# A two-layer decoder trunk: norm gains multiplied into prepared weights by GpSimd, and a reordered schedule

## The chip, the cores and the metric

The kernel runs on one core of a Trainium2 chip. The metric is device time in microseconds (us) of one execution; lower is better. The core's engines each run their own queue of instructions in program order: PE (TensorE, the matrix products), ACT (ScalarE), DVE (VectorE), POOL (GpSimd) and SP (SyncE, which here only issues DMA transfers). They meet only in semaphores: an instruction that waits holds up everything behind it on its engine.

## The reference

The input x is 1024 positions by 1024 features, mem is 256 by 1024. There are two layers, all in float32, and both have the same frame:

```
h = rms_norm(x, norm_gains[l, 0]); z = h @ w_in[l]
y_main = pool_mixer(z_main, ...)         # layer 0: sliding means over 2, 4, 8, 16 positions
y_main = dilated_mixer(z_main, shared)   # layer 1: 12 heads, rotary q, windows (128,1),(512,4),(2048,16)
y_mem  = memory_attn(z_mem, mem, mem_norm[l], w_mem_kv[l])   # 4 heads, kv = rms_norm(mem, g) @ w_mkv
y = concatenate([y_main, y_mem]) @ w_out[l];  x = x + rms_norm(y, norm_gains[l, 1])
h = rms_norm(x, norm_gains[l, 2]); gu = h @ w_gate_up[l]     # 1024 x 5632
y = (silu(gu[..., :D_FF]) * gu[..., D_FF:]) @ w_down[l];  x = x + rms_norm(y, norm_gains[l, 3])
# after layer 0: shared K, V = rope(rms_norm(x, kv_norm) @ w_kv), 1024 x 1536, one for all groups
```

`rms_norm(x, g)` is x over the root of its mean square, times the gains g, one for each feature. A gain can be multiplied into the rows of the weight matrix that follows instead of into x; the kernel does that for the matrices named below.

## The kernel before

**Precision.** Each factor of a matrix product is split into a high part H (the value rounded to the type fp32r) and a low part L = value - H, and a product is the sum of three matmuls, H*H, L*H and H*L. So each weight matrix that comes from memory needs two vector operations ahead of its first matmul: a copy with rounding (ACT, `WH<-WR` or `VH<-VR`) and a subtraction (DVE or POOL, `WL<-WR,WH` or `VL<-VR,VH`).

**Jobs.** The work of PE is a hand-written list of jobs (`plan_jobs`), one for each 128-wide stripe of an output: `mem` (memory keys and values), `in`, `kv`, `pool`, `out`, `ffn`, `st`, `down`. A job with a tag h covers one half (512) of the positions. A job's `slot` says where its weights lie in the shared weight space, and so when they can be loaded: once the previous user of the space is through. `HOOKS` lists the places k in a job at which one step of the attention (scores, softmax, transposes, values) is put between the job's matmuls.

**Norm statistics.** DVE sums the squares of x into `SS`; two small PE jobs called "col" (`PX<-CN,SS`, L688) and "row" (`PX<-CN,RC`, L697) turn them into the row `RSTD`. A wait of PE for `SS` is a wait for the last square to be summed. `mv` (L741) is PE's transposition of the memory values.

**FFN by Strassen's scheme.** Of the FFN's gate and up matrices the first stripes are ordinary `ffn` jobs; the other 18 stripes of each layer are 18 "pairs" (`st` jobs, `pair(l, f)`). A pair computes a 2x2 block product with 7 block products instead of 8. Each block product is 4 k-tiles of 3 matmuls, so a pair is 84 matmuls of 128x512 (L875, L876, L877). The weights of pair q+1 are prepared while PE works on pair q, in this order:

- `st_add(q+1)`, in layer 0 on DVE: four sums of blocks in `SR` (L1877 to L1880), the fourth ends `st_added`
- ACT: `st_raw_hi(q+1)` (L1252, 128x1536) rounds the plain blocks, `st_sum_hi(q+1)` (L1257, 128x2048) the sums; the second waits for `st_added`
- DVE: `st_raw_lo(q+1)` (L1887), `st_sum_lo(q+1)` (L1894), each after its high part; PE's first product of pair q+1 waits for the second

Between them DVE combines the block products of pair q as they end: u2 (L1900), c11 (L1906), u3 (L1911), c22 and v2 (L1917, L1918), c21 (L1922), c12 (L1927), each with one factor in PSUM, and ACT does the gate's nonlinearity in two halves (`silu_first` L1263, `silu_second` L1269).

**Prepared weights.** The 24 weight matrices (128x1024 each) of layer 1's `mem`, `in` and `kv` jobs are prepared during 16 of layer 0's 18 pairs, by turns one and two in a pair (`prepared(f)`), and stored back to memory. For each: SP loads it into one of three `VR` buffers, `keep_weight` on ACT multiplies in the gains `GN` (8 operations of 128x128, one for each k, L1141) and rounds it (L1144), POOL subtracts (L2390), SP stores `VH` and `VL`. POOL has no other work in layer 0's pairs. ACT's order in a pair is `p1_copy`, `silu_first`, `keep_weight` once or twice, `st_raw_hi(q+1)`, `st_sum_hi(q+1)`:

```
                    p1_copy(q)
                    if l == 0:
                        silu_first(q)
                        for i in prepared(f):
                            keep_weight(i)
                    if f < NF - 1:
                        st_raw_hi(q + 1)
                        st_sum_hi(q + 1)
```

**The other places that the change touches.** The start of layer 0: two `in` jobs (query stripes 6, 7), four `mem` jobs, then the pooled `in` jobs, with the memory attention in the hooks. The start of layer 1: `mem` jobs, for which the row `RSTDM` (the memory's norm) comes back from memory, then `in` jobs 6 and 7 in halves. Layer 1's output product in two parts (features 0 to 511 and 512 to 1023), with the rest of the attention in the hooks of part 0; the attention ends with a combination of its three groups (`combine_last`). Then layer 1's sublayer: `add_y` (L1848) adds the parts, `residual` (L1630) makes the new x, `scaled_low` (L1641) its low part `BL`, while PE is in `ffn` jobs, whose weights are split by ACT and DVE (`weight_lo`, L1578).

## Time and profile before

| what | value |
|---|---|
| time, median of 3 runs | 2398.61 us (2392.47 to 2398.93) |
| the profiled execution: its own time | 2402.4 us |
| its span | 2400.4 us |
| its mean granted clock of TensorE | 0.955 |
| PE busy | 2202.2 us, 92% |
| DVE busy | 1264.6 us, 53% |
| ACT busy | 944.5 us, 39% |
| POOL busy | 328.0 us, 14% |

PE is busy nearly all the time, so what can be gained without taking matmuls away is in PE's idle time and in the stretches in which its granted clock is below full. The profile gives for each idle stretch of an engine the instruction that ended it. The granted clock is one of two levels, 1.2 and 2.4 GHz; a value between them is a mean over a stretch.

### The profile page before, as it was taken

To read this page: it belongs to the slowest core of one execution; us is meant where nothing else is said; L and a number is where in the kernel's file an instruction comes from. 1 tells how busy PE (TensorE), PEld (TensorE's weight loads), DVE (VectorE), ACT (ScalarE), POOL (GpSimd) and SP (SyncE) were. 2 spreads that over 40 slices of the span, in tenths; PEclk is the share of its full clock that TensorE was granted. 3 is DMA by queue.
4 is the path that set the end of the run, shared out by engine and by line. 5 is a ranking of instruction groups with operands and counts; after the bars stand their busy time and mean duration, and the time that the engine had idled before them with its cause. 6 is when DMAs were issued, how large, how long until landed. Compare 5 with 4: busy or idle time off the path is not lost.

```text
span 2400.4 us, 25623 instructions
## 1 busy us (share of the span) xinstructions
PE 2202.2 (92%) x9718; PEld 1766.8 (74%) x9718; DVE 1264.6 (53%) x1901; ACT 944.5 (39%) x1575; POOL 328.0 (14%) x198
## 2 busy tenths in 40 slices
PE   6897999888888999998999997979799999999996
PEld 5675888776767778887777765657578888878885
DVE  6354375655565643525344445466656666672442
ACT  5335352434344433322444446653542222242421
POOL 3432100112111000000000014022222222200000
PEclk8998999999899999998999999989899999999998
DMA  4202232344444635554111101004212222263543
GB/s 160 73 14 90 88 121 75 142 184 149 179 148 173 222 117 199 163 174 182 53 64 43 59 30 36 19 17 154 75 53 79 79 79 82 94 216 97 197 132 104
DMA packets 83210, 265.10 MB, mean 110 GB/s; under 512 B 9360, under 2 KB 10640, under 8 KB 77840
## 3 DMA queue, kind: packets, MB, share of 16 engines
q1 hardware_dynamic: 66960, 234.10, 27.8%
q10 hardware_dynamic: 16128, 29.37, 3.6%
q8 instruction: 77, 1.26, 0.2%
q14 instruction: 45, 0.37, 0.0%
HBM read 195.14 MB, written 68.29 MB: 110 GB/s over the span
## 4 chain that ended last, share of the span: by engine, by line
PE 70%; DVE 12%; ACT 9%; issue 5%; DMA 3%; SPq 1%; POOL 0%; ACTq 0%; DVEq 0%
PE PS L662 8%; PE PS L875 7%; PE PS L877 7%; PE PS L876 7%; PE PS L663 7%; PE PS L665 7%; PE PS L895 6%; PE PS L897 6%; PE PS L896 6%; PE PSC L803 3%; ACT VR L1141 2%; PE PO L777 2%; DVE SL L1894 2%; PE PTR L787 1%; ACT VH L1144 1%
## 5 line engine op out<-in xcount | busy, mean ns | idle before, releaser
L895 PE MATMUL PS<-IH,DH 128*128 128x512 f32 x704 | 276.6, 393 | 6.5 <-DVE IL L1975 6.0
L897 PE MATMUL PS<-IH,DL 128*128 128x512 f32 x704 | 275.3, 391 | 0.0
L896 PE MATMUL PS<-IL,DH 128*128 128x512 f32 x704 | 275.3, 391 | 0.0
L875 PE MATMUL PS<-BH,SH 128*128 128x512 f32 x432 | 179.1, 415 | 54.7 <-DVE SL L1894 51.6
L875 PE MATMUL PS<-BHT,SH 128*128 128x512 f32 x576 | 225.8, 392 | 0.0
L876 PE MATMUL PS<-BLT,SH 128*128 128x512 f32 x576 | 224.2, 389 | 0.0
L877 PE MATMUL PS<-BHT,SL 128*128 128x512 f32 x576 | 224.2, 389 | 0.0
L876 PE MATMUL PS<-BL,SH 128*128 128x512 f32 x432 | 176.7, 409 | 0.0
L877 PE MATMUL PS<-BH,SL 128*128 128x512 f32 x432 | 176.7, 409 | 0.0
L895 PEld LDWEIGHTS PS<-IH,DH 128*128 128x128 f32 x704 | 132.9, 189 | 36.7 <-DVE IL L1975 8.5
L897 PEld LDWEIGHTS PS<-IH,DL 128*128 128x128 f32 x704 | 133.0, 189 | 27.9
L896 PEld LDWEIGHTS PS<-IL,DH 128*128 128x128 f32 x704 | 133.0, 189 | 27.5
L875 PEld LDWEIGHTS PS<-BH,SH 128*128 128x128 f32 x432 | 85.8, 199 | 79.6 <-DVE SL L1894 61.8
L1578 DVE TENSOR_TENSOR DL<-DR,DH 128x1408 fp32r<-128x1408 f32 x64 | 103.8, 1624 | 73.0 <-ACT DH L1004 73.0
L662 PE MATMUL PS<-XH,WH 128*128 128x512 f32 x320 | 138.8, 434 | 0.0
L663 PE MATMUL PS<-XL,WH 128*128 128x512 f32 x320 | 128.7, 402 | 0.0
L875 PEld LDWEIGHTS PS<-BHT,SH 128*128 128x128 f32 x576 | 109.4, 190 | 23.0
L876 PEld LDWEIGHTS PS<-BLT,SH 128*128 128x128 f32 x576 | 109.4, 190 | 23.0
L1613 DVE TENSOR_TENSOR SS<-SS,SCR 128x512 f32<-128x512 f32 x28 | 19.4, 691 | 202.6 <-ACT SCR L1031 202.6
L877 PEld LDWEIGHTS PS<-BHT,SL 128*128 128x128 f32 x576 | 108.1, 188 | 23.0
L662 PE MATMUL PS<-BH,WH 128*128 128x512 f32 x256 | 104.7, 409 | 20.9 <-DVE WL L1578 13.4
L2390 POOL TENSOR_TENSOR VL<-VR,VH 128x1024 fp32r<-128x1024 f32 x24 | 57.9, 2411 | 470.4 <-ACT VH L1144 470.4
(281 smaller groups left out, 4645.2 us busy)
## 6 DMA issues: line engine op xcount, KB each, us to landing
DR<-in_wdn SPq DMA_DIRECT2D x64, 704.0 KB, 4.1
SR<-in_wst SPq DMA_DIRECT2D x36, 1024.0 KB, 4.8
IR<-inner SPq DMA_DIRECT2D x88, 256.0 KB, 4.9
WR<-in_w SPq DMA_DIRECT2D x36, 512.0 KB, 4.6
inner<-TP SPq DMA_DIRECT2D x36, 512.0 KB, 2.6
VR<-in_w SPq DMA_DIRECT2D x24, 512.0 KB, 4.1
w_keep<-VH SPq DMA_DIRECT2D x24, 512.0 KB, 3.7
w_keep<-VL SPq DMA_DIRECT2D x24, 512.0 KB, 4.6
```

The source lines that it names most:

```text
L662: MM(out[h], wh[:, i, :], rh(h, k), start=(i == 0), stop=False)
L663: MM(out[h], wh[:, i, :], rl(h, k), start=False, stop=False)
L665: ins = MM(out[h], wl[:, i, :], rh(h, k), start=False, stop=last)
L803: MM(score_bank(a)[:, 0:nk], QF[rows, t, P * n:P * (n + 1)], keys, start=True, stop=True).then_inc(scored, 1)
L875: MM(BANK[bank], SH[b][:, w, c], BH[t][:, k, :], start=(k == 0), stop=False)
L876: MM(BANK[bank], SH[b][:, w, c], BL[t][:, k, :], start=False, stop=False)
L877: ins = MM(BANK[bank], SL[b][:, w, c], BH[t][:, k, :], start=False, stop=(k == 3))
L895: MM(bank, wh[:, i, :], IH[r][:, :], start=(k == 0), stop=False)
L896: MM(bank, wh[:, i, :], IL[r][:, :], start=False, stop=False)
L897: ins = MM(bank, wl[:, i, :], IH[r][:, :], start=False, stop=(k == NF - 1))
L1578: V.tensor_tensor(lo(j), raw(j), as_f32(hi(j)), ALU.subtract).then_inc(w_lo_dve, 1)
L2390: G_.tensor_tensor(VL[i % NV][:, :, :], VR[i % NV][:, :, :], as_f32(VH[i % NV][:, :, :]), ALU.subtract).then_inc(v_lo, 1)
```

## The change

Five parts. None changes what is computed, and the number of matmuls is the same.

1. **Prepared weights.** POOL multiplies the gains into a prepared weight, in one operation with `GN` broadcast along the row, ahead of its subtraction; ACT only rounds. On ACT `st_raw_hi(q+1)` moves ahead of `silu_first(q)`, and the second weight of a pair behind `st_sum_hi(q+1)`.
2. **Start of layer 0.** The first pooled `in` job moves ahead of the four `mem` jobs, with the norm's col and row hooks in it, and the squares ahead of the memory's split; the attention's hooks are spread anew; SP issues the loads of the next two `in` jobs behind the stores of the memory's parts.
3. **Start of layer 1.** `RSTDM` is loaded during the down product instead of behind two large loads; `mv` moves from the first half's `in` job 7 to the second half's.
4. **Output product of layer 1, part 0.** Attention steps: 4 in each job of the first half and 1 in each of the second (before 3 or 2, and 4, 4, 2, 2, 2, 2, 2, 1); the combination's pieces start earlier and are spread.
5. **Layer 1's sublayer.** `ffn` jobs get other slots, so that the first four weights are loaded and split during the output product's part 1; the product of y with the norm's row (16 operations, `y_norm`) moves from POOL to DVE (as in layer 0); the col and row hooks of x's second half move from the second `ffn` job of the second half to the first; pairs and down jobs of layer 1 use the weight space's regions in another turn.

```diff
@@ plan_jobs
             run = [Job("in", 0, m) for m in (6, 7)]
+            run += [Job("in", 0, POOL_IN[0])]
             run += [Job("mem", 0, m, gain=8) for m in range(4)]
-            run += [Job("in", 0, m) for m in POOL_IN]
+            run += [Job("in", 0, m) for m in POOL_IN[1:]]
...
-        jobs += [Job("ffn", l, (f, j), halves=(h,), tag=h, slot=wide(2 * f + j),
+        jobs += [Job("ffn", l, (f, j), halves=(h,), tag=h, slot=2 * f + j if l else wide(2 * f + j),
...
@@ attention steps
-        for m in range(NMT):
-            HOOKS[J[("in", 0, m, None)]] = (1, 3, 5, 7)
+        for n, m in enumerate(POOL_IN):
+            HOOKS[J[("in", 0, m, None)]] = () if n == 0 else (4, 5, 6, 7) if n == 1 else (1, 2, 4, 5, 7)
...
-            HOOKS[J[("out", 1, m, (0, 0))]] = (1, 2, 3) if m < 5 else (1, 3)
-            HOOKS[J[("out", 1, m, (0, 1))]] = (0, 1, 2, 3) if m < 2 else (1, 3) if m < 7 else (1,)
+            HOOKS[J[("out", 1, m, (0, 0))]] = (0, 1, 2, 3)
+            HOOKS[J[("out", 1, m, (0, 1))]] = (1,)
@@ PE
-                              (1, 0, 1): {3: [("col", s_x, 1)], 7: [("row", s_x, 1)]}}
+                              (1, 0, 0): {0: [("col", s_x, 1)], 4: [("row", s_x, 1)]}}
...
-                places = {0: [("col", 4, 1)], 3: [("row", 4, 1)]} if h else {4: [("mv", 1, 0)]}
+                places = {0: [("col", 4, 1)], 3: [("row", 4, 1)], 6: [("mv", 1, 0)]} if h else {}
@@ ACT keep_weight
-                act.wait_ge(v_loaded[b], 16 * (i // NV + 1))
-                for k in range(KT):
-                    ins = A(VR[b][:, k, :], VR[b][:, k, :], ACT.Copy, scale=GN[:, 8 * o.gain + k:8 * o.gain + k + 1])
-                    ins.then_inc(v_gained, 1)
-                act.wait_ge(v_gained, KT * (i + 1))
+                act.wait_ge(v_gained, i + 1)
                 A(VH[b][:, :, :], VR[b][:, :, :], ACT.Copy).then_inc(v_hi, 1)
@@ ACT pair
                     p1_copy(q)
+                    ready = prepared(f) if l == 0 else ()
+                    if len(ready):
+                        keep_weight(ready[0])
+                    if f < NF - 1:
+                        st_raw_hi(q + 1)
                     if l == 0:
                         silu_first(q)
-                        for i in prepared(f):
-                            keep_weight(i)
                     if f < NF - 1:
-                        st_raw_hi(q + 1)
                         st_sum_hi(q + 1)
+                    if len(ready) > 1:
+                        keep_weight(ready[1])
@@ DVE residual, layer 1
-                if r != 3:
-                    V.tensor_tensor(y, y, RSTD[:, c], ALU.mult).then_inc(y_normed[h], 1)
+                V.tensor_tensor(y, y, RSTD[:, c], ALU.mult).then_inc(y_normed[h], 1)
@@ DVE output product, part 0
+                    if (h, m) == (0, 7):
+                        combine_last(0)
+                        combine_last(1)
+                    if h and m in (1, 2, 4, 6):
+                        combine_last((2, 3, 4, 5)[(1, 2, 4, 6).index(m)])
...
@@ POOL
             for i in range(len(PRE)):
+                o = JOBS[PRE[i]]
+                pool.wait_ge(v_loaded[i % NV], 16 * (i // NV + 1))
+                G_.tensor_tensor(VR[i % NV][:, :, :], VR[i % NV][:, :, :], GN[:, 8 * o.gain:8 * o.gain + KT]
+                                 .unsqueeze(2).to_broadcast([P, KT, P]), ALU.mult).then_inc(v_gained, 1)
                 pool.wait_ge(v_hi, i + 1)
...
-            y_norm(0)
-            y_norm(1)
@@ SP
+                        sp.dma_start(RSTDM[:, :], rstd_keep).then_inc(mem_back, 16)
...
-            sp.dma_start(RSTDM[:, :], rstd_keep).then_inc(mem_back, 16)
```

The first place is ACT's queue in a pair of layer 0 with two prepared weights. Before (`SCR` is `p1_copy`; the rows of `TP` are `silu_first` and, last, the pair before's or this pair's `silu_second`; `VR_192` and `VR_193` are the two weights):

```order
L1279 ACTIVATE SCR_71<-PS 128x512
L1263 ACTIVATE TP_91<-TP_91 128x512
L1141 ACTIVATE VR_192<-VR_192,GN 128x128 x8
L1144 ACTIVATE VH_198<-VR_192 128x1024
L1141 ACTIVATE VR_193<-VR_193,GN 128x128 x8
L1144 ACTIVATE VH_199<-VR_193 128x1024
L1252 ACTIVATE SH_204<-SR_200 128x1536
L1257 ACTIVATE SH_204<-SR_200 128x2048
L1269 ACTIVATE TP_91<-TP_91 128x512
L1279 ACTIVATE SCR_71<-PS 128x512
```

The same place of the kernel after (all of its line numbers are higher; L1262 is the former L1252, L1267 the former L1257):

```order
L1289 ACTIVATE SCR_71<-PS 128x512
L1153 ACTIVATE VH_198<-VR_192 128x1024
L1262 ACTIVATE SH_204<-SR_200 128x1536
L1273 ACTIVATE TP_91<-TP_91 128x512
L1267 ACTIVATE SH_204<-SR_200 128x2048
L1153 ACTIVATE VH_199<-VR_193 128x1024
L1279 ACTIVATE TP_91<-TP_91 128x512
```

The rounding of the plain blocks (128x1536) stands behind one copy instead of behind sixteen gain operations, two copies and `silu_first`, and that of the sums (128x2048) ahead of the second weight.

The second place is POOL's queue in the same pairs. Before, the last two splits of ordinary weights (`WL`) and three prepared weights:

```order
L2347 TENSOR_TENSOR WL_141<-WR_115,WH_167 128x1024
L2347 TENSOR_TENSOR WL_142<-WR_116,WH_168 128x1024
L2390 TENSOR_TENSOR VL_194<-VR_191,VH_197 128x1024
L2390 TENSOR_TENSOR VL_195<-VR_192,VH_198 128x1024
L2390 TENSOR_TENSOR VL_196<-VR_193,VH_199 128x1024
```

After, the same stretch:

```order
L2377 TENSOR_TENSOR WL_141<-WR_115,WH_167 128x1024
L2377 TENSOR_TENSOR WL_142<-WR_116,WH_168 128x1024
L2424 TENSOR_TENSOR VR_191<-VR_191,GN 128x1024
L2427 TENSOR_TENSOR VL_194<-VR_191,VH_197 128x1024
L2424 TENSOR_TENSOR VR_192<-VR_192,GN 128x1024
L2427 TENSOR_TENSOR VL_195<-VR_192,VH_198 128x1024
L2424 TENSOR_TENSOR VR_193<-VR_193,GN 128x1024
L2427 TENSOR_TENSOR VL_196<-VR_193,VH_199 128x1024
```

Each subtraction now has the product with the gains ahead of it, in the same buffer.

The third place is PE's queue at the start of the second half of layer 1's `ffn` jobs. Before, in the second job (`BH_223` and `BH_224` are k = 0 to 3 and 4 to 7 of the second half's x, `WH_170` the second job's weight):

```order
L662 MATMUL PS<-BH_223,WH_170 128x512
L663 MATMUL PS<-BL_231,WH_170 128x512
L665 MATMUL PS<-BH_223,WL_144 128x512
L688 MATMUL PX<-CN,SS 128x1 x4
L662 MATMUL PS<-BH_224,WH_170 128x512
```

After, in the first job (`WH_165` is its weight, `WH_172` that of the first half's last job):

```order
L669 MATMUL PS<-BH_222,WH_172 128x512
L670 MATMUL PS<-BL_230,WH_172 128x512
L672 MATMUL PS<-BH_222,WL_146 128x512
L669 MATMUL PS<-BH_223,WH_165 128x512
L670 MATMUL PS<-BL_231,WH_165 128x512
L672 MATMUL PS<-BH_223,WL_139 128x512
L695 MATMUL PX<-CN,SS 128x1 x4
L669 MATMUL PS<-BH_223,WH_165 128x512
```

The col hook (`PX<-CN,SS`) moved ahead by 11 k-steps of three matmuls: PE now meets it behind the second half's first k-step.

## Rows read from the trace of the kernel before

**Rows 1.** The page, a group of instructions: busy us, mean ns, idle before, releaser.
```profile
L875 PE MATMUL PS<-BH,SH 128*128 128x512 f32 x432 | 179.1, 415 | 54.7 <-DVE SL L1894 51.6
```

**Rows 2.** Chain that ended last, layer-0 pairs: start us, us, what.
```profile
430.81 2.21 DVE SL L1894
...
789.38 2.21 DVE SL L1894
```

**Rows 3.** Windows: us, then busy (x instructions) PE PEld DVE ACT POOL, clock, DMA share, GB/s.
```profile
430.81:789.38 358.57, 309.25 (x1264) 249.00 (x1262) 199.90 (x226) 153.92 (x282) 55.45 (x23) 0.93 0.44 163
2000.00:2100.00 100.00, 100.00 (x443) 82.81 (x442) 64.38 (x64) 26.33 (x22) 25.81 (x20) 1.00 0.25 90
```

**Rows 4.** Timeline, PE at two pair starts: start us, us, instruction [idle before <-releaser].
```profile
480.74 0.50 PE L875 MATMUL PS<-BH,SH 128*128 128x512 f32 x1 [1.50 <-DVE SL L1894]
...
505.01 0.80 PE L875 MATMUL PS<-BH,SH 128*128 128x512 f32 x1 [4.94 <-DVE SL L1894]
```

**Rows 5.** Timeline, ACT within the pair that starts at 480.74.
```profile
490.48 2.44 ACT L1141 ACTIVATE VR<-VR,GN 128x128 f32<-128x128 f32 x8
492.96 1.06 ACT L1144 ACTIVATE VH<-VR 128x1024 fp32r<-128x1024 f32 x1
...
497.35 1.47 ACT L1252 ACTIVATE SH<-SR 128x1536 fp32r<-128x1536 f32 x1
498.73 1.90 ACT L1257 ACTIVATE SH<-SR 128x2048 fp32r<-128x2048 f32 x1
```

**Rows 6.** Timeline, DVE within the same pair.
```profile
492.00 0.69 DVE L1880 TENSOR_TENSOR SR<-SR 128x512 f32<-128x512 f32 x1
...
498.86 2.70 DVE L1887 TENSOR_TENSOR SL<-SR,SH 128x1536 fp32r<-128x1536 f32 x1 [5.56 <-ACT SH L1252]
...
502.68 2.28 DVE L1894 TENSOR_TENSOR SL<-SR,SH 128x2048 fp32r<-128x2048 f32 x1
```

**Rows 7.** Groups of instructions by line, POOL: busy us, mean ns, idle before.
```profile
L2390 POOL TENSOR_TENSOR VL<-VR,VH 128x1024 fp32r<-128x1024 f32 x24 | 57.9, 2411 | 470.4 <-ACT VH L1144 470.4
...
L2422 POOL TENSOR_TENSOR YOA<-YOA,RSTD 128x512 f32<-128x512 f32 x16 | 25.4, 1619 | 73.8 <-ACT RSTD L1022 73.8
...
L2341 POOL TENSOR_TENSOR WR<-WR,GN 128x1024 f32<-128x1024 f32 x4 | 9.5, 2387 | 19.2 <-DVE XLA L1597 19.2
```

**Rows 8.** Timeline, POOL within the same pair.
```profile
497.53 2.42 POOL L2390 TENSOR_TENSOR VL<-VR,VH 128x1024 fp32r<-128x1024 f32 x1 [1.02 <-ACT VH L1144]
```

**Rows 9.** Source lines, DVE: count, duration ns min/median/max, first and last start.
```profile
L1887 DVE TENSOR_TENSOR SL<-SR,SH x36: 1750/1756/2700, 399.0 to 2107.4; 128x1536 fp32r<-128x1536 f32 x36
...
L1605 DVE TENSOR_TENSOR SS<-SS,TP x7: 1212/2729/3185, 28.3 to 41.8; 128x1024 f32<-128x1024 f32 x7
```

**Rows 10.** Timeline, PE at the start of layer 0.
```profile
44.58 1.87 PE L688 MATMUL PX<-CN,SS 128*128 128x1 f32 x8 [7.05 <-DVE SS L1605]
...
72.44 0.76 PE L803 MATMUL PSC<-KM,QF 64*128 64x256 f32 x1 [5.90 <-ACT VM L1087]
```

**Rows 11.** Timeline, PE at the start of layer 1.
```profile
1084.90 0.58 PE L728 MATMUL PSC<-MH,WH 128*128 128x256 f32 x1 [3.16 <-DMA RSTDM<-rstd_keep]
...
1115.87 1.11 PE L741 MATMUL PX<-CN,MV 128*128 128x128 f32 x4 [4.74 <-DVE MV L1692]
```

**Rows 12.** Timeline, PE ahead of layer 1's first output products.
```profile
1616.60 0.77 PE L662 MATMUL PS<-CH,WH 128*128 128x512 f32 x1 [8.92 <-DVE CL L1814]
```

**Rows 13.** Timeline, PE in layer 1's FFN, first half.
```profile
1717.44 0.79 PE L662 MATMUL PS<-BH,WH 128*128 128x512 f32 x1 [9.91 <-DVE WL L1578]
...
1728.69 0.50 PE L662 MATMUL PS<-BH,WH 128*128 128x512 f32 x1 [3.23 <-DVE WL L1578]
```

**Rows 14.** Timeline, DVE in the same stretch.
```profile
1712.16 1.75 DVE L1630 SCALAR_TENSOR_TENSOR YOA<-YOA,GN,TP 128x512 f32<-128x512 f32 x1
...
1719.23 0.74 DVE L1630 SCALAR_TENSOR_TENSOR YOA<-YOA,GN,TP 128x512 f32<-128x512 f32 x1
...
1729.15 0.68 DVE L1613 TENSOR_TENSOR SS<-SS,TP 128x512 f32<-128x512 f32 x1
```

More of the change, by code:

```diff
@@ L820, in _ @@
             job(J[("in", 0, 7, None)], xh, xl)
-            memory_job(0, 0, hook=at_k({6: [("col", 0, 0), ("col", 0, 1)]}))
-            memory_job(0, 1, hook=at_k({4: [("row", 0, 0), ("row", 0, 1)], 7: [("mcol", 0, 0)]}))
-            memory_job(0, 2, hook=at_k({6: [("mrow", 0, 0)]}))
+            job(J[("in", 0, POOL_IN[0], None)], xh, xl,
+                hook=at_k({3: [("col", 0, 0)], 4: [("col", 0, 1)], 7: [("row", 0, 0), ("row", 0, 1)]}))
+            memory_job(0, 0, hook=at_k({1: [("mcol", 0, 0)]}))
+            memory_job(0, 1, hook=at_k({3: [("mrow", 0, 0)]}))
+            memory_job(0, 2)
             memory_job(0, 3)
@@ L827, in _, with hook @@
                 j = J[("in", 0, m, None)]
-                def hook(i, first=n == 0, places=HOOKS[j]):
-                    if first and i == 0:
+                if n == 0:
+                    continue
+                def hook(i, first=n == 1, places=HOOKS[j]):
+                    if first and i == 2:
                         memory_values(0, 0)
@@ L1163, in _ @@
                     weight_hi(1)
+            weight_hi(2)
+            for k in range(KT):
+                square0(k)
             act.wait_ge(tables_in, MEM_IN)
@@ L1462, in _ @@
             sub_layer(0)
-            for k in range(6):
-                residual(2, 1, k)
-            memory_values(1)
-            for k in range(6, KT):
+            for k in range(KT):
                 residual(2, 1, k)
@@ L1493, in combine @@
                 else:
-                    for g, t in enumerate(tiles):
-                        act.wait_ge(cmb_out, 3 * pair + g + 1)
-                        A(CH[:, t, :], OF[:, t, :], ACT.Copy).then_inc(c_hi, 1)
+                    act.wait_ge(cmb_out, 3 * pair + g + 1)
+                    A(CH[:, tiles[g], :], OF[:, tiles[g], :], ACT.Copy).then_inc(c_hi, 1)
             def split_memory(m):
@@ L1514, in _ @@
                         step()
-                    if (n, q) in ((15, 4), (16, 1), (17, 1)):
-                        combine(0, n - 15)
+                    if n == 15 and 2 <= q <= 4:
+                        combine(0, "exp", q - 2)
+                    if (n, q) == (16, 1):
+                        combine(0, "inverse")
+                    if n == 17 and q <= 2:
+                        combine(0, "split", q)
                     if n and i != 1 and q < 4:
@@ L1765, in _, with pooled_input @@
             query0(7)
+            def pooled_input(n):
+                j = J[("in", 0, POOL_IN[n], None)]
+                dve.wait_ge(mm_done, j + 1)
+                if n == 0:
+                    dve.wait_ge(pads_zero, 3)
+                    for h in range(2):
+                        ins = V.tensor_tensor(T[0][:, HALF[h]], BANK[banks(j)[h]], RSTD[:, HALF[h]], ALU.mult)
+                    ins.then_inc(in_scaled, 1)
+                else:
+                    V.tensor_tensor(T[0], PS[j % 2][:, :], RSTD[:, :], ALU.mult).then_inc(in_scaled, 1)
+            pooled_input(0)
             for m in range(4):
@@ L2274, in combine_last @@
                 else:
-                    for n, t in enumerate(tiles):
-                        split_low(t, 18 + n + 1)
-                    split_low(7, 22)
+                    split_low(tiles[part - 5], 18 + part - 4)
             for n in range(19):
@@ L2362, in _ @@
             pool.wait_ge(x0_lo, KT)
-            gain(POOL_JOBS[0])
-            weights_to(first + 3)
+            weight_lo(POOL_JOBS[0])
+            done[0] += 1
+            pool.wait_ge(ss0_done, KT)
+            gain(POOL_JOBS[1])
+            weights_to(J[("in", 0, POOL_IN[3], None)])
             pool.wait_ge(pads_zero, 3)
@@ L2416, in _ @@
             weights_to(NJ)
-            def y_norm(h):
-                pool.wait_ge(px_free, px_at[("row", 5, h)])
-                for k in range(KT):
-                    G_.tensor_tensor(YO[h][:, k, :], YO[h][:, k, :], RSTD[:, HALF[h]],
-                                     ALU.mult).then_inc(y_normed[h], 1)
             def st_add(q):
-                b = SR[q % 2]
+                b = SR[pair_slot(q)]
                 pool.wait_ge(*st_seen(q))
```

132 lines of the change are left out of this document (68 added, 64 removed).

## The prediction

> **What bounds the kernel now.** I read the page first: PE is busy 92% of the span, so only its idle and half-clock stretches can be won. The costliest idle entry of the page is PE's wait at the first product of a pair, 54.7 us, of which 51.6 us ended with DVE's `st_sum_lo`, L1894 [rows 1]. The chain of waits says the same for layer 0: `st_sum_lo` stands in it 16 times, from 430.81 to 789.38, so 15 pairs take 358.57 us, 23.90 us each [rows 2]. The windows give what a pair should take: in layer 1, 443 matmuls in 100.00 us without any idle time, so 84 matmuls are 18.96 us; in layer 0 the mean granted clock is 0.93 over the pairs, against 1.00 there [rows 3]. A layer-0 pair thus loses 4.94 us, and there are 16 with weights to prepare.
>
> The timeline divides the loss. PE waits 1.50 us ahead of the pair that starts at 480.74 and 4.94 us ahead of the next, at 505.01, where its first matmul takes 0.80 us instead of 0.50 [rows 4]. The two waits make 6.4 of the 9.9 us that two pairs lose; the other 3.5 us are matmuls at the half clock after the long wait.
>
> Why `st_sum_lo` is late is read inside the pair that starts at 480.74, one with two weights. ACT gives them 2 x (2.44 + 1.06) = 7.0 us from 490.48 on, and only then, at 497.35 and 498.73, rounds the next pair's blocks (1.47 and 1.90 us) [rows 5]. DVE had its sums ready at 492.7, then idled 5.56 us for ACT, did `st_raw_lo` in 2.70 us and `st_sum_lo` at 502.68, 21.9 us after the pair's start [rows 6]. So ACT's order and its eight small gain products are the cause.
>
> **Part 1, the pairs.** Counted from the pair's first product (t = 0). ACT no longer does the gains: of 3.5 us for a weight 1.06 stay. The rounding of the plain blocks comes behind one copy and is done long before DVE asks. The sums are ready at 492.69 - 480.74 = 11.95 [rows 6]; ACT rounds them in 1.90 [rows 5], to about 13.9. DVE meanwhile has u3 and `st_raw_lo`, which takes 1.76 us alone and took up to 2.70 [rows 9], to about 15; then c22 and v2, then `st_sum_lo` from 15.9. The 2.28 us of it [rows 6] end at 18.2, ahead of 18.96: no stall, if nothing else is in its way.
>
> What is in its way is POOL. Its load in a two-weight pair is now 4 operations of 2.4 us (the subtraction's mean is 2411 ns; the nearest row for the product with broadcast gains is L2341's, the same shape, 2387 ns [rows 7]), 9.6 us of 19. The trace shows what two engines do to each other: the only `st_raw_lo` that take 2.70 instead of 1.76 us are those beside a POOL subtraction, as at 498.86 beside the one that runs from 497.53 to 499.95: 1.08 us of overlap, 0.94 us longer [rows 6, 8, 9]. The square sums L1605 take 1.21 us at best and 2.73 in the median where POOL works beside them [rows 9]. So a DVE operation with two SBUF inputs waits for a POOL operation that is under way. In a two-weight pair ACT's second copy now stands behind the sums' rounding, 13.9 + 1.06 = 14.9, and POOL's second subtraction runs from there to 17.4. `st_sum_lo`, ready at 15.9, would end at 17.4 + 2.3 = 19.7 or somewhat later: a stall of 0.7 to 1.0 us. In a one-weight pair POOL's 4.8 us mostly lie earlier: 0 to 0.6 us. The long wait that brought the half clock is gone, so those 3.5 us for two pairs go too. I take 19.4 us for the mean pair: 16 x (23.9 - 19.4) = **-72 us**. Bounds: no contention at all, 16 x 4.94 = -79; every other pair pays a whole further POOL operation (2.4 us) and some half clock, 21.0 us on the mean, -46.
>
> The Trainium skill's page "SBUF — State Buffer", section "Who interferes with whom", gives this a rule: the port that DVE uses for a second SBUF input is shared with GpSimd, and is held exclusively by an instruction that has it. By it `st_sum_lo` waits out the whole subtraction, as I took it; the trace agrees with its 0.94 us of delay for 1.08 us of overlap. The same rule speaks against this change, since it doubles GpSimd's share of the port in these pairs; what it could cost at most is the second rival.
>
> **Part 2, start of layer 0.** PE waits 7.05 us for the square sums and 5.90 us for the memory values [rows 10]. After, the first pooled `in` job (about 11 us at full clock) fills the first wait, and the memory products come later; but two `in` weights are now loaded only behind the memory's stores, and PE will wait for the next job's weight, I estimate 8 us, from the load's place in SP's queue. I lay out both orders to the point where PE resumes: 72.4 before with 7/8 of the pooled job to do, about 72 after with all of it done. That gives -10 less a half-clock stretch: **-8 us**; bounds 0 (waits only renamed) and -13 (both waits gone).
>
> **Part 3, start of layer 1.** The 3.16 us wait for `RSTDM` falls to the 1 to 1.5 us that the memory's own reload takes, and the 4.74 us wait of `mv` goes, as `MV` is then long ready [rows 11]; each also had matmuls at half clock behind it. Against that, the col hook of the second half's first `in` job, which `mv` no longer delays, meets the squares of x about 4 us early. **-6 us**, bounds -2 and -9.
>
> **Part 4, output product.** PE waits 8.92 us for the last low part of the attention's output (`CL`) [rows 12], at the end of a chain that starts only with the last attention steps. With four steps a job in the first half the chain starts about two jobs earlier, some 10 us, so this wait and some 6 us of smaller ones in the hooks before it go, while denser steps give back a little: **-15 us**, bounds -9 (only the one wait) and -20.
>
> **Part 5, layer 1's sublayer.** The waits for `WL` of 9.91 and 3.23 us go [rows 13], since the first four weights are split an output part earlier. POOL's `y_norm` took 1.62 us each [rows 7], and beside it DVE's `residual` took 1.75 instead of 0.74 us [rows 14]; on DVE the 16 products are some 11 us, which the faster `residual` and `scaled_low` (16 x 2 x 1.0, at most) pay for. So the second half's x comes at about the same time as before, its last square at 1729.2 [rows 14], which after is met by a col hook that PE reaches 11 k-steps (about 7 us) sooner [order of PE, third place], with PE's waits gone besides: a new wait of 7 to 8 us and some half clock after it. Together 13.1 + 6 (smaller waits, half clock) + 13 (the row's values, and with them the chain into the pairs, no longer wait on late hooks) less 11: **-21 us**, bounds -8 and -28.
>
> **Sum.** -72 - 8 - 6 - 15 - 21 = -122 us. The profiled execution's own time is 2402.4, 3.8 above the median of the runs, 2398.61. So 2280 in its terms, 2277 in the median's; I say **2278 us**. With the bounds of part 1 and half of those of the others this case spans 2262 to 2296.
>
> **The rivals.**
> - *Contention is dearer* (0.18). If POOL's product or subtraction meets the four sums as well (they have two SBUF inputs, and end at 11.95), everything behind them slips by up to 2.4 us, and `st_sum_lo` by another 2.4: pairs of 21.5 us, a gain of 38 instead of 72 us, 2312 us. For it: the doubled POOL time. Against: the sums come at a point where the first subtraction is done.
> - *Only the pairs gain* (0.14): in parts 2 to 5 each wait that goes is replaced by the next in line, as the new waits on `in` weights and squares already suggest. 2402 - 72 - 12 = 2318, less 4: 2314 us.
> - *Better than forecast* (0.07): no stall in the pairs, and parts 2 to 5 at their far bounds: -79 - 13 - 9 - 20 - 28 = -149, 2250 us.
> - *The change doesn't do what it says in the pairs* (0.04): ACT, with its copy ahead of the plain blocks, waits there for POOL's product, because a weight lands late; pairs stay near 23.9, and only the rest gains: 2350 us. Against: ACT found its weight there at 490.48 with no wait, and a weight is loaded a pair ahead.
> - *Slower* (0.02): POOL and DVE become the bound of a pair. The price is the sum of what excludes one another: 9.6 us of POOL, 2.9 of sums, 1.8 + 2.3 of low parts and 0.7 of the product, some 17 us; with DVE's seven PSUM operations of 0.7 added as if nothing overlapped, 22.6. It turns the sign only where the pair takes over 23.9 + 50/16 = 27 us, that is if POOL's product took 7 us or more instead of 2.4, say by a slow form of the broadcast: 2402 + 16 x 5 = above 2420 with the other parts at nothing. L2341 has the same form at 2.387 us [rows 7], which is why I give it so little.
>
> **How the numbers follow.** The forecast has 0.55. From 2252 to 2320 the range holds it, most of the two rivals with 0.18 and 0.14 and some of the better case; 0.15 is left out. A measurement of this kernel can tell about 0.3% (7 us) from no change. All cases but the last are faster by more than that; same has 0.01, slower 0.02.
>
> **What the profile after would show.** Right: PE's wait on `st_sum_lo` falls from 51.6 to under 15 us, the pairs' chain has a period near 19.4, the granted clock in them is near 1.0; `st_sum_lo` at about 4 us instead of 2.3 in every other pair; POOL's new product near 2.4 us; no wait on `WL` or `CL`, but waits of 7 to 8 us on an `in` weight at the start and on `SS` in the ffn jobs. Wrong: sums of 2 us instead of 0.7 (first rival), ACT idle ahead of its first copy (fourth), waits of the same sum under other names in parts 2 to 5 (second). What I am least sure of is parts 4 and 5, where many short waits and the clock's answer to them make up the term.

## The result and the profile after

| | before | after |
|---|---|---|
| time, median | 2397.72 us (2392.47 to 2398.93, 4 runs) | 2289.61 us (2289.42 to 2291.11, 4 runs) |
| ratio | | 0.9554, 95% interval 0.9538 to 0.9571 |
| span of the profiled execution | 2400.4 us | 2287.3 us |
| mean granted clock of TensorE | 0.955 | 0.977 |

The change saved 108 us. From the page of the kernel after, the busy times of the engines and the row that answers to [rows 1]:

```profile
PE 2163.1 (95%) x9718; PEld 1739.8 (76%) x9718; DVE 1269.6 (56%) x1918; ACT 888.4 (39%) x1383; POOL 363.2 (16%) x206
...
L888 PE MATMUL PS<-BH,SH 128*128 128x512 f32 x432 | 170.2, 394 | 5.5 <-DVE SL L1923 5.5
```

PE's wait at a pair's first product fell from 54.7 to 5.5 us, and its busy time from 2202 to 2163 us with the same 9718 matmuls, because fewer ran at the half clock of 1.2 GHz: the mean granted clock rose from 0.955 to 0.977.

The spans differ by 113 us, 5 more than the medians, because the profiled execution of the kernel before was 4.7 us above its median (2402.4 against 2397.72). Where the 113 us came from is read by cutting both traces at the same matmuls. In layer 0 a stage begins with the first product of its kind: "start" is all up to layer 0's output product, "pairs 0" begins with the first product of the pairs and ends with the first of the down product. "Down 0 and start 1" reaches to the first dilated score of layer 1, "attention" from there to the last `in` product. From there on a stage begins with the last product of the kind before it, so "pairs 1" begins with the last ffn product. The same cuts in every run serve the experiments below (us):

| stage | before | after | difference |
|---|---|---|---|
| start | 220.9 | 217.3 | -3.6 |
| layer 0, output and ffn | 191.5 | 191.6 | +0.1 |
| **pairs 0** | 420.8 | 353.4 | **-67.4** |
| down 0 and start 1 | 374.6 | 368.8 | -5.8 |
| attention | 279.6 | 273.7 | -5.9 |
| output 1 | 172.4 | 164.2 | -8.2 |
| ffn 1 | 124.6 | 108.7 | -15.9 |
| pairs 1 | 348.7 | 342.8 | -5.9 |
| down 1 | 267.3 | 266.8 | -0.5 |

The pairs first. Their stage in the windows of before and of after (length, busy PE, granted clock, then DMA):

```profile
412.40:833.20 420.80, 368.75 (x1514) 0.94 0.47 171
```

```profile
408.90:762.30 353.40, 347.48 (x1513) 1.00 0.56 204
```

PE's idle time fell by 46 us (52.1 to 5.9), and its busy time by 21 us at a clock that is now full. The chain of waits holds `st_sum_lo` (now L1923) only in every other pair, the ones with two weights:

```profile
448.78 4.08 DVE SL L1923
...
487.41 4.08 DVE SL L1923
...
719.31 4.08 DVE SL L1923
```

From 448.78 to 719.31 are 14 pairs, 19.32 us each, against 23.90 in [rows 2]. Within a pair with two weights, DVE's timeline (the fourth sum, `st_raw_lo`, `st_sum_lo`; last, `st_sum_lo` of the next pair, which has one weight) and then POOL's:

```profile
444.63 0.69 DVE L1909 TENSOR_TENSOR SR<-SR 128x512 f32<-128x512 f32 x1
...
445.83 1.75 DVE L1916 TENSOR_TENSOR SL<-SR,SH 128x1536 fp32r<-128x1536 f32 x1
...
448.70 4.15 DVE L1923 TENSOR_TENSOR SL<-SR,SH 128x2048 fp32r<-128x2048 f32 x1
...
468.29 3.05 DVE L1923 TENSOR_TENSOR SL<-SR,SH 128x2048 fp32r<-128x2048 f32 x1
```

```profile
438.03 2.40 POOL L2427 TENSOR_TENSOR VL<-VR,VH 128x1024 fp32r<-128x1024 f32 x1 [12.41 <-ACT VH L1153]
440.38 1.89 POOL L2424 TENSOR_TENSOR VR<-VR,GN 128x1024 f32<-128x1024 f32 x1
448.30 2.41 POOL L2427 TENSOR_TENSOR VL<-VR,VH 128x1024 fp32r<-128x1024 f32 x1 [6.02 <-ACT VH L1153]
450.65 3.95 POOL L2424 TENSOR_TENSOR VR<-VR,GN 128x1024 f32<-128x1024 f32 x1
```

These answer to [rows 6] and [rows 8]. `st_raw_lo` follows the sums without idle time; before, DVE idled 5.56 us for ACT there. But `st_sum_lo`, started at 448.70 when POOL's subtraction of 448.30 was under way, took 4.15 instead of 2.28 us: POOL's ended at 450.71, and 450.71 + 2.28 = 452.99, where it ended at 452.85. POOL's next product, which takes 1.89 us when alone (440.38), in its turn took 3.95. The `st_sum_lo` of the pairs with one weight is delayed as well, to 2.84 to 3.76 us from 468.29 to 700.19: at 468.29 it met POOL's product for the next weight, under way from 467.29 to 469.19. PE doesn't wait for it there, so only the other pairs stand in the chain. PE at the starts of two pairs, against [rows 4]:

```profile
431.88 0.80 PE L888 MATMUL PS<-BH,SH 128*128 128x512 f32 x1 [3.73 <-DVE SL L1923]
...
452.90 0.50 PE L888 MATMUL PS<-BH,SH 128*128 128x512 f32 x1 [0.22 <-DVE SL L1923]
```

The steady wait, at each later pair start that waits, is 0.22 us; only the first wait of the series has 3.73 us, more than the 1.50 us of [rows 4]. The waits of the other parts in PE's timeline, in order of time, against [rows 10 to 13]:

```profile
68.44 0.80 PE L669 MATMUL PS<-XHA,WH 128*128 128x512 f32 x1 [6.31 <-POOL WL L2377]
...
115.66 0.44 PE L794 MATMUL PTR<-CN,PR 128*128 128x128 f32 x2 [1.83 <-DVE PR L1740]
...
1013.01 0.39 PE L735 MATMUL PSC<-MH,WH 128*128 128x256 f32 x1 [2.63 <-DMA ML<-mem_keep]
...
1048.48 0.72 PE L695 MATMUL PX<-CN,SS 128*128 128x1 f32 x5 [3.72 <-DVE SS L1632]
...
1526.45 0.47 PE L669 MATMUL PS<-CH,WH 128*128 128x512 f32 x1 [1.07 <-POOL WL L2377]
...
1529.28 0.50 PE L669 MATMUL PS<-CH,WH 128*128 128x512 f32 x1 [0.51 <-DVE CL L1843]
...
1599.67 0.59 PE L695 MATMUL PX<-CN,SS 128*128 128x1 f32 x2 [3.30 <-DVE SS L1632]
...
1630.87 1.44 PE L695 MATMUL PX<-CN,SS 128*128 128x1 f32 x6 [4.89 <-DVE SS L1632]
```

At the start the waits of 7.05 and 5.90 us went, one of 6.31 us for the low part of the second pooled job's weight came, and the denser hooks now wait 1.83 us for a probability tile at a time. The wait for `RSTDM` became one of 2.63 us for the memory's low parts, and `mv`'s 4.74 us became 3.72 us for the squares. The 8.92 us for `CL` became 1.07 + 0.51. The waits of 9.91 and 3.23 us for `WL` went, and the squares of both halves of x are waited for, 3.30 and 4.89 us.

### The profile page after: what moved, and what is told of

Same layout as the page of the kernel before. It is cut to its first block, busy times and chain, and to the rows that moved or that the text cites. A ratio compares the mean times of both kernels' runs of the same rounds, so it can differ in the third digit from the quotient of the medians.

```text
span 2287.3 us, 25459 instructions
## 1 busy us (share of the span) xinstructions
PE 2163.1 (95%) x9718; PEld 1739.8 (76%) x9718; DVE 1269.6 (56%) x1918; ACT 888.4 (39%) x1383; POOL 363.2 (16%) x206
## 4 chain that ended last, share of the span: by engine, by line
PE 78%; DVE 11%; ACT 4%; issue 4%; DMA 3%; SPq 0%; POOL 0%; ACTq 0%; DVEq 0%
PE PS L669 8%; PE PS L888 8%; PE PS L889 8%; PE PS L890 8%; PE PS L670 7%; PE PS L672 7%; PE PS L908 7%; PE PS L910 6%; PE PS L909 6%; PE PSC L812 3%; PE PO L784 2%; DVE SL L1923 2%; PE PTR L794 1%; DMA TP<-x_mid 1%; DVE SS L1632 1%
## 5 line engine op out<-in xcount | busy, mean ns | idle before, releaser
L908 PE MATMUL PS<-IH,DH 128*128 128x512 f32 x704 | 276.5, 393 | 5.7 <-DVE IL L2004 5.2
L888 PE MATMUL PS<-BH,SH 128*128 128x512 f32 x432 | 170.2, 394 | 5.5 <-DVE SL L1923 5.5
L889 PE MATMUL PS<-BL,SH 128*128 128x512 f32 x432 | 168.9, 391 | 0.0
L890 PE MATMUL PS<-BH,SL 128*128 128x512 f32 x432 | 168.6, 390 | 0.0
L1632 DVE TENSOR_TENSOR SS<-SS,SCR 128x512 f32<-128x512 f32 x28 | 19.4, 692 | 203.0 <-ACT SCR L1044 203.0
L888 PEld LDWEIGHTS PS<-BHT,SH 128*128 128x128 f32 x576 | 108.1, 188 | 22.6
L1730 DVE CUSTOM_DVE_ANT_0 PSC<-PSC,MK 128x128 f32<-128x128 f32 (+1 forms) x88 | 32.2, 366 | 157.1 <-PE PSC L812 157.0
L2377 POOL TENSOR_TENSOR WL<-WR,WH 128x1024 fp32r<-128x1024 f32 (+2 forms) x40 | 81.1, 2040 | 197.2 <-ACT WH L1017 197.2
L1267 ACT ACTIVATE SH<-SR 128x2048 fp32r<-128x2048 f32 x36 | 69.1, 1920 | 106.4 <-POOL SR L2462 67.9
```

The lines of the kernel that those rows point to most:

```text
L888: MM(BANK[bank], SH[b][:, w, c], BH[t][:, k, :], start=(k == 0), stop=False)
L889: MM(BANK[bank], SH[b][:, w, c], BL[t][:, k, :], start=False, stop=False)
L890: ins = MM(BANK[bank], SL[b][:, w, c], BH[t][:, k, :], start=False, stop=(k == 3))
L908: MM(bank, wh[:, i, :], IH[r][:, :], start=(k == 0), stop=False)
L1267: A(SH[pair_slot(q)][:, S3:, :], SR[pair_slot(q)][:, S3:, :], ACT.Copy).then_inc(st_hi, 1)
L2377: G_.tensor_tensor(lo(j), raw(j), as_f32(hi(j)), ALU.subtract).then_inc(w_lo_pool, 1)
```

## The experiments

All were timed beside the kernel before on the same chip. "Pairs 0" and so on are the stages of the table above, read from the profiled execution of each.

**1. Does the pairs' part stand alone?** The kernel before with part 1 whole.

> The kernel before with part 1 alone (gains on POOL, new order on ACT; start, layer 1 and everything else as before). Theory: the five parts add up, and the pairs are worth what the two traces show between the first matmul of the pairs and the first of the down product, 67 us: 2397.7 - 67 = 2331 us, within 5. Rival, the parts help one another (loads or clock): under 2322 or above 2340.

2329.19 us (ratio 0.9711, 0.9695 to 0.9727); pairs 0: 352.9 us, all other stages within 1 us of before. So the pairs are worth 68 us alone and 67 in the whole change: the parts add.

**2. Was it the order or the gains?** The kernel before with this alone:

```diff
                     p1_copy(q)
+                    ready = prepared(f) if l == 0 else ()
+                    if len(ready):
+                        keep_weight(ready[0])
+                    if f < NF - 1:
+                        st_raw_hi(q + 1)
                     if l == 0:
                         silu_first(q)
-                        for i in prepared(f):
-                            keep_weight(i)
                     if f < NF - 1:
-                        st_raw_hi(q + 1)
                         st_sum_hi(q + 1)
+                    if len(ready) > 1:
+                        keep_weight(ready[1])
```

> The kernel before with ACT's new order in the pairs alone; ACT still multiplies the gains in 8 operations, POOL only subtracts. Theory A, the order was the cause: the first weight takes ACT 3.5 us before t = 7, the sums are rounded at 13.9 to 14.5, the second weight's 3.5 us lie behind it, and POOL's subtraction of it comes after the sums' low part, so pairs of 18.96 to 19.1 us, a saving of 70 to 74 us: 2326 us. Rival B, the gains' 2.44 us on ACT were the cause: pairs stay above 22 us, 2365 us or more.

2321.16 us (ratio 0.9676, 0.966 to 0.9692); pairs 0: 344.4 us, 8.5 less than with the gains on POOL as well. PE waits for `st_sum_lo` only once in the whole stage, and no instance of it (L1898 here: count, ns min/median/max, first and last start) is delayed:

```profile
434.08 0.50 PE L875 MATMUL PS<-BH,SH 128*128 128x512 f32 x1 [0.66 <-DVE SL L1898]
```

```profile
L1898 DVE TENSOR_TENSOR SL<-SR,SH x36: 2279/2284/2286, 404.2 to 2028.9; 128x2048 fp32r<-128x2048 f32 x36
```

18 pairs at 18.96 us are 341.3, so nearly nothing is left to gain. The steady pairs take 19.04 us each, by the starts of `st_sum_lo` (14 pairs from 449.80 to 716.35). Theory A holds: the new order suffices, and ACT has room for the gains. That the products' time on ACT had no part in the old delay does not follow; experiment 4 bears on that.

**3. The gains on POOL without the order.** The kernel before with `keep_weight` and POOL's loop as after, ACT's pair as before.

> The kernel before with the gains on POOL and ACT's old order. Theory A: the sums' rounding slips only by two copies (2.1 us) and the plain blocks' by the same, but POOL's subtractions now fall beside the sums and the low parts on DVE: pairs of about 21 and 19 us by turns, 20.2 in the mean, 2397.7 - 16 x 3.7 = 2339 us. Rival B, the gains were all of it: 2330 us or less.

2403.72 us, a ratio of 1.0024 (1.0013 to 1.0035): slightly slower than before. Pairs 0: 424.8 us. Both theories missed. ACT's timeline in a pair with two weights (two copies, then the plain blocks and the sums), POOL's and DVE's (third and fourth sum, `st_raw_lo`, `st_sum_lo`):

```profile
494.43 1.04 ACT L1140 ACTIVATE VH<-VR 128x1024 fp32r<-128x1024 f32 x1
500.50 1.06 ACT L1140 ACTIVATE VH<-VR 128x1024 fp32r<-128x1024 f32 x1 [5.03 <-POOL VR L2387]
501.47 1.47 ACT L1248 ACTIVATE SH<-SR 128x1536 fp32r<-128x1536 f32 x1
502.84 1.89 ACT L1253 ACTIVATE SH<-SR 128x2048 fp32r<-128x2048 f32 x1
```

```profile
495.55 2.62 POOL L2390 TENSOR_TENSOR VL<-VR,VH 128x1024 fp32r<-128x1024 f32 x1 [15.94 <-ACT VH L1140]
498.13 2.34 POOL L2387 TENSOR_TENSOR VR<-VR,GN 128x1024 f32<-128x1024 f32 x1
501.64 2.40 POOL L2390 TENSOR_TENSOR VL<-VR,VH 128x1024 fp32r<-128x1024 f32 x1 [1.17 <-ACT VH L1140]
```

```profile
495.22 0.69 DVE L1875 TENSOR_TENSOR SR<-SR 128x512 f32<-128x512 f32 x1
495.94 2.77 DVE L1876 TENSOR_TENSOR SR<-SR 128x512 f32<-128x512 f32 x1
...
502.97 2.69 DVE L1883 TENSOR_TENSOR SL<-SR,SH 128x1536 fp32r<-128x1536 f32 x1 [3.66 <-ACT SH L1248]
...
506.78 2.79 DVE L1890 TENSOR_TENSOR SL<-SR,SH 128x2048 fp32r<-128x2048 f32 x1
```

ACT waits 5.03 us ahead of its second copy, for a product with the gains (498.13) that stands on POOL behind the first subtraction (495.55); and behind ACT's second copy stand the roundings. The fourth sum, beside POOL's subtraction, took 2.77 instead of 0.69 us.

**4. The same with POOL's products one weight ahead,** to take ACT's wait away: the product of weight i+1 is issued before the subtraction of weight i.

> As the run with POOL's gains and ACT's old order, but POOL multiplies the next weight's gains before it subtracts the present one, so that ACT never waits for them. Theory A, ACT's 5.03 us wait for the second product with the gains, behind POOL's first subtraction, undid the change there: pairs of about 21 and 19 us by turns, 2397 - 59 = 2339 us, at most 2355. Rival B, the port is what costs (sums and low parts on DVE delayed by POOL whatever its order): 2380 us or more.

2349.15 us (ratio 0.9805, 0.9785 to 0.9825); pairs 0: 376.7 us. So of the 80 us of the pairs between experiments 3 and 2, POOL's own order held 48. Against the kernel before, the pairs are 44 us shorter with ACT's order left as it was: the gain products on ACT were a good part of the delay, and moving them off ACT takes away more than half of it without reordering ACT. DVE's timeline shows what the port held of the rest:

```profile
489.56 2.78 DVE L1876 TENSOR_TENSOR SR<-SR 128x512 f32<-128x512 f32 x1
...
492.87 3.25 DVE L1883 TENSOR_TENSOR SL<-SR,SH 128x1536 fp32r<-128x1536 f32 x1
...
497.24 3.27 DVE L1890 TENSOR_TENSOR SL<-SR,SH 128x2048 fp32r<-128x2048 f32 x1
```

Against 0.69, 1.75 and 2.28 us alone these are 4.6 us more in one pair. Theory A holds for the most part; the mean pair was (376.7 - 344.4)/16 = 2.0 us above the one of experiment 2. How much of that is the port and how much ACT's old order is not separated.

**5. The gains back on ACT in the kernel after,** in the new order.

> The kernel after with the gains back on ACT (8 operations each), in the new order. Theory A: with the order right ACT has room for them, and the 0.36 us a pair that POOL's port use costs goes: 2289.6 - 6 = 2284 us, st_sum_lo at 2.28 us throughout. Rival B: without POOL's product the pairs fall back to above 22 us: 2335 us or more. Rival C, both fit and contention costs nothing: 2289 to 2291 us.

2280.3 us (ratio 0.9513, 0.9498 to 0.9527), 9 us less than the kernel after, the intervals apart. Pairs 0: 344.2 against 353.4 us, every other stage within 2 us, and `st_sum_lo` never delayed:

```profile
L1927 DVE TENSOR_TENSOR SL<-SR,SH x36: 2279/2284/2286, 400.6 to 1989.8; 128x2048 fp32r<-128x2048 f32 x36
```

Of the 9.2 us, 4 are the 14 steady pairs, 19.04 us each as in experiment 2 instead of 19.32; the rest is the first wait, 0.62 instead of 3.73 us, with the half clock behind it. Theory A holds, with a saving of 9 us where 6 were expected.

**6. POOL's second subtraction moved out of DVE's way.** The kernel after, in which POOL does

```diff
+                f, n = next((f, list(prepared(f)).index(i)) for f in range(NHT, NF) if i in prepared(f))
+                if n:
+                    pool.wait_ge(st_lo, 2 * (f - NHT + 2))
                 pool.wait_ge(v_hi, i + 1)
```

> The kernel after; POOL waits for the sums' low part on DVE before it subtracts the second weight of a pair. Theory A, the port is all that the steady pairs still lose (0.22 us of PE's wait and the lateness behind it in every other pair): st_sum_lo takes 2.28 us everywhere, pairs of 18.96 us, 2289.6 - 15 x 0.36 = 2284 us. Rival B: POOL's work, pushed into the next pair, makes ACT wait for the next product with the gains ahead of the plain blocks, and the pairs grow: 2295 us or more.

2283.19 us (ratio 0.9526, 0.9512 to 0.954). Pairs 0: 349.0 us, 4.4 less than after. Of all waits of PE for `st_sum_lo` the first alone is left:

```profile
433.63 0.73 PE L888 MATMUL PS<-BH,SH 128*128 128x512 f32 x1 [3.77 <-DVE SL L1923]
```

The steady pairs take 19.04 us here too (14 pairs from 450.56 to 717.12), so the steady loss was the overlap with POOL's second subtraction, and it could be moved away without undoing anything: theory A. Its other half missed: `st_sum_lo` takes 2.28 us only in the pairs with two weights, and still 2.79 to 3.40 us in the others, where PE doesn't wait for it.

**7. The products with the norm's row back on POOL,** in the kernel after (layer 1's `y_norm`).

> The kernel after with the 16 products of y with the norm's row in layer 1 back on POOL. Theory A, the move to DVE pays, as residual beside POOL took 1.75 instead of 0.74 us: 5 to 10 us slower, 2295 to 2300 us, the waits for SS longer than 3.30 and 4.89 us. Rival B, DVE's 11 us and POOL's contention are worth the same: 2288 to 2291 us. Rival C: DVE is the bound there and POOL takes work off it: 2285 us or less.

2294.6 us (ratio 0.9575, 0.9559 to 0.9591). Ffn 1: 111.2 against 108.7 us. PE's wait for the second half's squares grew from 4.89 to

```profile
1633.19 1.86 PE L695 MATMUL PX<-CN,SS 128*128 128x1 f32 x8 [7.89 <-DVE SS L1632]
```

so theory A holds in sign, with 2.5 us by the stage. The medians differ by 5 us, but the intervals of the two ratios overlap (0.9538 to 0.9571 for the kernel after).

**8. The hooks of x's second half back in the second job,** in the kernel after.

> The kernel after with the col and row hooks of x's second half where they were, in the second ffn job of the second half. Theory A, the earlier hook only made a wait: PE's 4.89 us for SS go, and some of the 6.8 us at half clock behind it, and nothing later waits for the row: 2289.6 - 5 to 8 = 2283 us. Rival B: the row comes some 7 k-steps later, the chain into the pairs is late and PE waits at the first pair for as much: 2289 us or more.

2295.94 us (ratio 0.958, 0.9563 to 0.9596). The wait for the second squares went, as theory A says, and others came, as B says:

```profile
1646.49 0.65 PE L704 MATMUL PX<-CN,RC 128*128 128x128 f32 x4 [0.57 <-DVE RC L1602]
...
1665.88 0.77 PE L669 MATMUL PS<-BH,WH 128*128 128x512 f32 x1 [2.38 <-DVE TP L1857]
...
1686.61 0.76 PE L888 MATMUL PS<-BH,SH 128*128 128x512 f32 x1 [2.69 <-DVE TP L1870]
```

Ffn 1 and pairs 1 together: 105.6 + 347.0 = 452.6, against 108.7 + 342.8 = 451.5 us after. The hook's place is worth 1 us, little more than the same stages vary by in two executions of the kernel after (experiment 11). The rest of the 6 us of the median doesn't come from it: the trace of this run is already 8.5 us behind at the end of output 1, in stages that the edit doesn't touch.

**9. The `in` weight's load ahead of the memory's stores** in SP's queue, in the kernel after.

> The kernel after with the load of the second pooled in job's weight ahead of the stores of the memory's parts in SP's queue. Theory A: PE's wait of 6.31 us for the weight's low part at 68.44 goes or falls under 2 us, with the half clock behind it: 2280 to 2284 us. Rival B: the load waits for its buffer anyway, and the stores wait behind it: 2288 us or more.

2286.07 us (ratio 0.9539, 0.9522 to 0.9556). The start is 212.8 us, 4.5 less, and the wait of 6.31 us is gone. The time fell by less than theory A's 2280 to 2284 us and stayed under rival B's 2288; its interval overlaps that of the kernel after, so by the medians alone nothing is shown.

**10. Both edits of 5 and 9 together.**

> The kernel after with both edits that helped it: gains on ACT in the new order (saved 9) and the second pooled in job's load ahead of the memory's stores (saved 3.5 to 4.5). Theory, they lie in stages of their own and add: 2289.6 - 13 = 2276 us, first stage near 213 us, pairs of layer 0 near 344 us. Rival, the clock takes back what the start gains: 2280 us.

2278.57 us (2274.33 to 2285.16; ratio 0.9506, 0.9478 to 0.9534), the lowest of all, but no less than experiment 5 alone by what can be measured. Pairs 0: 344.6 us; the start, though, took 217.7. The wait of 6.31 us is gone here too. The same two stretches of the start's attention, by windows (busy PE, granted clock), in experiment 9 and then in this one:

```profile
133.66:154.18 20.52, 18.68 (x89) 1.00 0.04 10
154.18:178.24 24.06, 16.88 (x79) 0.92 0.05 17
```

```profile
133.49:155.59 22.10, 20.26 (x89) 0.92 0.03 10
155.59:182.79 27.20, 20.02 (x78) 0.82 0.05 15
```

The matmuls are the same, and the waits ahead of them are too (1.84 and 7.18 us), but the second run had a lower granted clock and took 4.7 us longer. That the load's move saves 4.5 us is thus shown up to 134 us of the run, and what reaches the end is not settled.

**11. The kernel after once more, as a control.**

> The kernel after, unchanged, as a control beside the others: 2288 to 2292 us. Theory: in stages that nothing touches, such as layer 1's attention stage (273.7 us in its first trace, 273 to 280 in the other runs), the time varies by some us with where the clock falls, so an edit's worth is read by its stage.

2290.12 us (2288.22 to 2293.18; ratio 0.9558, 0.9542 to 0.9574), each stage within 0.7 us of the first trace. The attention stage, which no edit touches, took 273.7 and 274.1 us in it, 279.6 to 279.7 in the kernel before and in experiments 1, 3 and 12, 277.6 in experiment 8, 276.5 in experiment 4, 275.7 in experiment 2, and 273.3 to 274.5 in the others.

**12. Two pieces of part 5 alone:** the kernel before with the products on DVE and the hook in the first job.

> The kernel before with two pieces of part 5 alone: the 16 products with the norm's row on DVE, and the col and row hooks of x's second half in the first job. The weights' slots and the order of their splits stay. Theory A, the slots are what part 5 rests on: the waits for WL stay, and DVE has 11 us more ahead of them, so layer 1's ffn stage is not shorter than 124.6 us and the time 2397 to 2403. Rival B, the products and the hook give half of the 22 us by themselves: 2388 us.

2384.4 us (ratio 0.9952, 0.9936 to 0.9968). Ffn 1 is 119.5 (-5.1) and pairs 1 342.8 (-5.9) us, 11.0 together: rival B, theory A falls. The waits for `WL` stay, but 9.91 + 3.23 became

```profile
1709.12 0.79 PE L662 MATMUL PS<-BH,WH 128*128 128x512 f32 x1 [4.27 <-DVE WL L1578]
...
1723.27 0.80 PE L662 MATMUL PS<-BH,WH 128*128 128x512 f32 x1 [7.07 <-DVE WL L1578]
```

In ffn 1, DVE with the 16 products of its own is thus not later than before. In pairs 1, PE's wait of 3.10 us at the first pair (at 1788.31 in the trace before) is gone, with the half clock behind it. Which of the two pieces does what is not separated here; in the kernel after, taking back the one cost 2.5 us (experiment 7) and the other 1 (experiment 8). What is left for the slots and the order of the splits is the other half, 21.8 - 11.0 = 10.8 us, by subtraction; no run has them alone.

## Why the prediction was right, and where it was not

The forecast of 2278 us (range 2252 to 2320) met 2289.6. It was 11.6 us too low. The terms make 8.9 of that (-122 forecast, -113.1 by the spans); most of the rest is that the forecast took off 3.8 us for a profiled execution above the median, while the profiled execution of the kernel after lay at its median. The terms:

- **Pairs: -72, measured -67.4.** The period was forecast as 19.4 and is 19.32 us. `st_sum_lo` runs into POOL's second subtraction and waits it out, as worked out: 4.15 us instead of 2.28. The sum took 16 savings of 4.5 us, and 15 came: from the first wait at a pair's start to the last are 15 pairs, 358.6 us before and 291.6 after. In the series' first pair all of POOL's work is late, its weight landing only then, and meets DVE's four sums; that pair grew from 20.7 to 23.0 us. The forecast had not looked at it. Its sums in DVE's timeline, three of them at 2.3 to 2.8 instead of 0.69 us:

```profile
417.91 2.37 DVE L1906 TENSOR_TENSOR SR<-SR 128x512 f32<-128x512 f32 x1
420.31 0.69 DVE L1907 TENSOR_TENSOR SR<-SR 128x512 f32<-128x512 f32 x1
421.04 2.82 DVE L1908 TENSOR_TENSOR SR<-SR 128x512 f32<-128x512 f32 x1
423.89 2.27 DVE L1909 TENSOR_TENSOR SR<-SR 128x512 f32<-128x512 f32 x1
```

  ACT, too, waited there for the late product ahead of its first copy, the forecast's sign of the fourth rival, in this pair alone:

```profile
419.76 1.06 ACT L1153 ACTIVATE VH<-VR 128x1024 fp32r<-128x1024 f32 x1 [7.30 <-POOL VR L2424]
```

  POOL's product takes 1.90, not 2.4 us, where nothing disturbs it. The forecast's 2387 ns [rows 7] was a mean: two of its four instances took 1.90 us, and the two beside DVE's square sums 2.88. In the pairs with one weight POOL's work did not lie earlier, as taken: their `st_sum_lo` was delayed too, but by so little that PE did not wait.
- **"ACT's order and its eight small gain products are the cause" holds, but the cure needed only the order.** Experiment 2 has the eight products still on ACT and the best time of the pairs, 76 us less than before. Experiment 4 has them off ACT in the old order and saves 44 us, so they were part of the delay; experiment 3, with POOL's items in the order of the kernel after, saves nothing. Once the order is right, moving the gains to POOL costs 9 us (experiments 1 against 2, and 5). The sum came out right because it took the order and the cost of the port together. The Trainium skill's page "SBUF — State Buffer", section "Who interferes with whom", was named as what speaks against the change; the trace agrees with its rule (DVE's 4.15 us), and experiment 5 shows that this half of the change is worse than none.
- **Start: -8, measured -3.6.** The wait for the `in` weight was forecast (8 us, measured 6.31). Mis-sized was what five jobs cost that take the hooks of six: waits of 1.83 us where there were 0.47.
- **Start of layer 1: -6, measured -4.8,** and 1.0 more in the down product: as forecast, with the col hook's wait at 3.72 us for the 4 us forecast.
- **Output 1: -15, measured -8.2.** The wait for `CL` went as forecast. What failed is the further 6 us of smaller waits in the hooks and the clock. The stage in the windows of before and of after (length, busy PE):

```profile
1487.80:1660.20 172.40, 147.44 (x663) 0.92 0.13 43
```

```profile
1405.20:1569.40 164.20, 147.81 (x663) 0.95 0.19 62
```

  Idle time fell by 8.6 us (25.0 to 16.4), 7.3 of them at the wait for `CL` (8.92 to 1.07 + 0.51); the smaller waits stayed, in other places.
- **Layer 1's sublayer: -21, measured -21.8** (ffn 1 and pairs 1). The new wait for the squares was forecast as 7 to 8 us and is 4.89, with one of 3.30 us for the first half that the forecast did not have. Experiment 12 says that the right sum came in part by luck. The forecast gave 19 us to the waits for `WL` and the smaller ones, and to the products and the hook only 13 less 11, that is 2; the two pieces alone gave 11.0, and 10.8 are left for the rest.
- **Attention: 0, measured -5.9.** Not the change's doing by any wait: nearly the same idle time (19.1 and 18.8 us) and the same 1209 matmuls at a granted clock of 0.98 instead of 0.95. This is luck: without it the terms would have been 15 us too high, not 9.

Of the rivals, the dearer contention was seen in that first pair, and throughout in experiments 3 and 4, where POOL's work falls on the sums; ACT's wait for a POOL product (the fourth rival) was seen for a late load in the first pair, and in every other pair of experiment 3 for POOL's own order. Had the change left ACT's order as it was, the pairs would have gained nothing (experiment 3: 4 us slower).

Three of the prediction's figures don't follow from its own numbers, none with a bearing on the forecast. The upper end of its case, 2296 us, should be about 2320 by the bounds that it names (26 us for part 1 and half of 8 + 4 + 6 + 13); the 22.6 us of the last rival add up to 22.2; and the chances, with the 0.01 for "same", to 1.01.

## What to carry to other kernels

When an engine's work in a loop delays what the bottleneck waits for, first try to move that work behind the critical operations in the same queue; here that alone gave 77 us. Moving it to another engine as well brought a loss of 9 us here, where the first engine had room (what it is worth where there is none was not tried), and on GpSimd it has a price in the DVE operations with two SBUF inputs that start while a GpSimd operation is under way. An engine that takes over one step of a chain (product, copy elsewhere, subtraction) must issue the next item's first step ahead of this item's last, or the in-order queue undoes the move (48 us in the pairs between experiments 3 and 4, 55 us in the whole time).

## What the runs showed of the hardware

- A DVE operation with both inputs in SBUF and a POOL operation on SBUF excluded each other, and they took turns: `st_sum_lo` waited for the subtraction under way (4.15 for 2.28 us), and POOL's next product, already issued, waited for `st_sum_lo` (3.95 for 1.89 us). A DVE operation with one input in PSUM was not held up: u2 (L1929) at 439.13, beside POOL's subtraction of 438.03 to 440.43, took its usual 0.69 us, as all 36 of its kind did.
- POOL's 128x1024 product with a factor broadcast along the row takes 1.90 us where nothing disturbs it, the subtraction of two full tiles 2.41. The 2.39 us of [rows 7] for the broadcast product are the mean of 1.90, 1.90, 2.88 and 2.88 us; the two long ones lie beside DVE's square sums of 2.7 to 3.2 us.
- The same matmuls behind the same waits differ by up to 3.1 us in a stretch of 24 (24.06 and 27.20) with a granted clock of 0.92 and 0.82, and by 6 us in the attention stage from one kernel to another. Why the clock fell differently is open. Edits worth under some 6 us were read from their own stage for that reason.
